# A mixture-of-experts layer whose expert rows are added in memory, the last block by a product

## The reference

```python
def moe_ffn(h, w_router, b_router, w_gate_up, b_gate_up, w_down, b_down):
    logits = (h @ w_router).astype(jnp.float32) + b_router
    topv, idx = lax.top_k(logits, TOP_K)            # 4 of 32 experts for each token
    gates = jax.nn.softmax(topv, axis=-1)
...
    def expert_block(args):
        xblk, e = args
        gu = xblk @ w_gate_up[e] + b_gate_up[e]
        gate = jnp.minimum(gu[:, :D_FF], SWIGLU_LIMIT)
        up = jnp.clip(gu[:, D_FF:], -SWIGLU_LIMIT, SWIGLU_LIMIT)
        act = (up + 1.0) * (gate * jax.nn.sigmoid(SWIGLU_ALPHA * gate))
        return act @ w_down[e] + b_down[e]
...
    out = jnp.zeros((t, d), jnp.float32).at[tbuf].add(ybuf.astype(jnp.float32) * wbuf[:, None])
    return out
...
        h2 = rmsnorm(x, norm_ffn_g).reshape(b * s, d)
        ff = moe_ffn(h2, w_router, b_router, w_gate_up, b_gate_up, w_down, b_down)
        x = x + ff.reshape(b, s, d).astype(x.dtype)
```

## Time and profile before

| | |
|---|---|
| three executions | 3075.31, 3075.50, 3072.84 us |
| median | 3075.31 us |
| profiled execution | 3074.51 us, its span 3072.7 us |
| TensorE busy | 2839.8 us (92% of the span) |
| VectorE busy | 1196.2 us (39%) |
| ScalarE busy | 802.5 us (26%) |
| GpSimd busy | 116.7 us (4%) |
| moved by DMA | 578.08 MB |
| granted TensorE clock, mean | 0.979 of full speed |

### The profile page before, as it was taken

The page is one execution under the profiler, slowest core; times in us unless marked ns, Lnnn a source line. Parts: engine busy times, 40 slices in busy tenths (PEclk is TensorE's granted clock), DMA queues, the critical chain, the costliest instruction groups (busy, mean ns, idle before and its releaser), DMA issues.

```text
span 3072.7 us, 42784 instructions
## 1 busy us (share of the span) xinstructions
PE 2839.8 (92%) x15464; PEld 1695.2 (55%) x15465; DVE 1196.2 (39%) x2551; ACT 802.5 (26%) x1607; POOL 116.7 (4%) x132
## 2 busy tenths in 40 slices
PE   8989889998999989899889779999999999999999
PEld 7874567753333333233333368575676596676774
DVE  6770674323212222122221166435333355444432
ACT  3221661111322222222222223423111224323111
POOL 0000100000000000000000000011000000110000
PEclk9999999997999999999999989999999999999999
DMA  4222002237999999999999552021321331122221
GB/s 175 83 69 69 15 1 96 83 138 298 395 419 401 425 426 403 418 395 411 423 406 397 205 200 97 28 93 36 102 83 55 99 101 55 54 74 76 82 69 69
DMA packets 119627, 578.08 MB, mean 188 GB/s; under 512 B 13933, under 2 KB 19437, under 8 KB 85712
## 3 DMA queue, kind: packets, MB, share of 16 engines
q1 hardware_dynamic: 110000, 559.37, 46.9%
q0 software_dynamic: 9504, 17.07, 1.5%
HBM read 572.97 MB, written 20.97 MB: 193 GB/s over the span
## 4 chain that ended last, share of the span: by engine, by line
PE 79%; DMA 11%; DVE 5%; ACT 2%; issue 2%; DVEq 1%; POOLq 0%; ACTq 0%; SPq 0%
PE banks L399 28%; PE banks L1547 11%; DMA arena<-in_w_up 10%; PE banks L336 8%; PE banks L1088 7%; PE banks L1588 5%; PE banks L841 4%; PE banks L1555 3%; PE banks L819 3%; PE banks L854 2%; PE banks L830 2%; PE banks L1594 2%; PE banks L275 1%; DVE arena L907 1%; PE banks L1527 1%
## 5 line engine op out<-in xcount | busy, mean ns | idle before, releaser
L399 PE MATMUL banks<-arena 128*128 128x256 f32 (+2 forms) x4256 | 916.3, 376 | 18.4 <-ACT arena L436 7.9
L399 PEld LDWEIGHTS banks<-arena 128*128 128x128 f32 x4256 | 795.7, 191 | 128.6 <-issue 21.9
L1547 PE MATMUL banks<-arena 128*64 128x512 f32 x2048 | 476.3, 610 | 67.8 <-DMA arena<-in_w_up 49.8
L1547 PEld LDWEIGHTS banks<-arena 128*64 128x64 f32 x2048 | 154.3, 139 | 343.8 <-issue 341.7
L436 ACT ACTIVATE arena<-banks 128x512 f32<-128x512 f32 (+2 forms) x152 | 89.1, 587 | 622.2 <-PE banks L399 622.2
L336 PE MATMUL banks<-arena 128*128 128x512 f32 x576 | 250.0, 592 | 0.0
L1588 PE MATMUL banks<-arena 128*64 128x512 f32 x1024 | 236.1, 599 | 0.0
L1689 DVE TENSOR_TENSOR arena<-banks,arena 128x512 f32<-128x512 f32 x64 | 44.3, 692 | 486.6 <-PE banks L1573 261.3
L452 DVE TENSOR_TENSOR arena<-banks,arena 128x512 f32<-128x512 f32 (+2 forms) x114 | 77.3, 678 | 383.2 <-PE banks L399 381.7
L1088 PE MATMUL banks<-arena 128*128 128x512 f32 x512 | 222.9, 592 | 3.7 <-DVEq L205 3.7
L384 DVE TENSOR_TENSOR arena<-arena 128x1024 f32<-128x1024 f32 (+2 forms) x152 | 182.4, 1200 | 21.8 <-issue 19.4
(11 more groups left out here) (218 smaller groups left out, 2389.1 us busy)
## 6 DMA issues: line engine op xcount, KB each, us to landing
arena<-in_w_up SPq DMA_DIRECT2D x128, 2048.0 KB, 23.4
arena<-in_w_down SPq DMA_DIRECT2D x128, 1024.0 KB, 21.5
arena<-in_w_in SPq DMA_DIRECT2D x76, 1024.0 KB, 5.0
arena<-in_w_out SPq DMA_DIRECT2D x12, 1024.0 KB, 5.0
arena<-in_w_branch SPq DMA_DIRECT2D x24, 512.0 KB, 4.7
arena<-expert_rows SPq DMA_DIRECT2D x4, 2048.0 KB, 14.5
arena<-in_w_in SPq DMA_DIRECT2D x2, 2048.0 KB, 10.0
arena<-in_w_in SPq DMA_DIRECT2D x4, 832.0 KB, 4.4
```

Source lines behind the costliest of these rows:

```text
L399: last = PE.matmul(PS[:, bank, t * width:(t + 1) * width], one[:, t * P:(t + 1) * P], other, start=(first and t == 0 and kk == 0), stop=(t ...
L1547: last = PE.matmul(PS[HB * s:HB * (s + 1), 4 + h], xT[:, k, 0:HB], gate_up(2 * h + s, k), start=(k == 0), stop=(k == 7))
```

## The change

The table of expert rows in memory is gone. In its place stands `x_sums`, 512 rows. The router stage writes x there. In the loop VectorE multiplies the rows of a block by their gates, and GpSimd adds them to `x_sums` with an indirect DMA whose operation is an addition, indexed by token. The last block isn't written: its rows lie in partitions 0 to 95 of `Y_`, the biases of the second matmul in partitions 96 to 127, and a matrix `SEL` holds in the same partitions the gate of each row at its token and the gates of all 32 experts for each token. One product with 128 steps for each half tile gives the contribution of the last block and of all biases. SyncE loads the sums back into `x3` once the write of the last block but one has landed, and VectorE adds the product. The gates of the list rows (`GLIST`) come from a second product of 16 steps in the router stage. The combine stage has no fence. Gathers and writes name 96 rows in place of 128.

```diff
-        YD = nc.dram_tensor("expert_rows", [S * TOPK, D], F32, kind="Internal").ap()
+        XD = nc.dram_tensor("x_sums", [S, D], F32, kind="Internal").ap()
...
+                sp.dma_start(v(Y_, D, NE, BS), A["b_down"]).then_inc(SEM["bdown_in"], 16)
...
-            G.indirect_dma_start(out=v(XG, D), out_offset=None, in_=H2D,
-                                 in_offset=bass.IndirectOffsetOnAxis(ap=v(TOK, 1).bitcast(U32), axis=0),
+            G.indirect_dma_start(out=v(XG, D, BS), out_offset=None, in_=H2D,
+                                 in_offset=bass.IndirectOffsetOnAxis(ap=v(TOK, 1, BS).bitcast(U32), axis=0),
...
             def pe_(pe, c):                                   # router stage
-                    last = PE.transpose(PS[0:NE, 3, tt * P:(tt + 1) * P], Gm[:, tt], ident)
+                    last = PE.matmul(PS[BS:P, 3, tt * P:(tt + 1) * P], Gm[:, tt], ident, start=True, stop=True, tile_position=(0, BS))
                 last.then_inc(SEM["gt_mm"], 1)
-                pe.wait_ge(SEM["gt_rdy"], up(1))
-                pe.wait_ge(SEM["bdown_in"], 16)
-                down_biases(0, 4)
-                down_biases(1, 6)
...
-                down_biases(2, 2)
-                pe.wait_ge(SEM["table_rdy"], up(1))
-                down_biases(3, 0)
+                for a_ in range(16):
+                    if a_ % 4 == 0:
+                        pe.wait_ge(SEM["gate_rows"], up(a_ // 4 + 1))
+                    last = PE.matmul(PS[0:BS, 2, 0:LISTS], gate_rows[:, a_], slots[:, a_].rearrange("p b e -> p (b e)"),
+                                     start=(a_ == 0), stop=(a_ == 15))
+                last.then_inc(SEM["gates_listed"], 1)
...
             def act_(act, c):                                 # router stage
+                for tt in range(TT):
+                    act.wait_ge(SEM["addr_rdy"], up(tt + 1))
+                    for a_ in range(4 * tt, 4 * tt + 4):
+                        last = AC.activation(gate_rows[:, a_], rows_at[:, a_, 0:BS], ACT.Copy, scale=per_slot[:, a_:a_ + 1])
+                    last.then_inc(SEM["gate_rows"], 1)
...
+                sp.dma_start(XD.rearrange("(t p) d -> p t d", p=P), x3).then_inc(SEM["sums_in"], 16)
...
             def sp_(sp, c):                                   # expert stage, behind its loop
                 sp.wait_ge(SEM["all_out"], up(1))
+                for tt in range(TT):
+                    sp.dma_start(x3[:, tt], XD[tt * P:(tt + 1) * P, :]).then_inc(SEM[f"comb{tt}"], 16)
+                sp.wait_ge(SEM["act_rdy"], up(2 * final + 2))
+                sp.wait_ge(SEM["gathered"], 16 * final + 32)
...
             def pe_(pe, c):                                   # expert stage
-                pe.wait_ge(SEM["bias_added"], up(2))
                 gather_T(1)
-                pe.wait_ge(SEM["bias_added"], up(4))
-                with pe.Fori(0, nb) as j:
+                pe.wait_ge(SEM["gt_rdy"], up(1))
+                pe.wait_ge(SEM["gates_out"], up(1))
+                with pe.Fori(0, final + 1) as j:
+                    few = entry(pe, FEW, j, 1)
                     pe.wait_ge(SEM["xt_free"], up(j + 1))
-                    few = entry(pe, FEW, j, 1)
...
+                pe.wait_ge(SEM["y_rdy"], up(final + 1))
+                for tt in range(TT):
+                    for n in range(2):
+                        last = PE.matmul(PS[:, SUMS[tt] + n], v(SEL + P * tt, P), v(Y_ + 512 * n, 512), start=True, stop=True)
+                    last.then_inc(SEM["comb_mm"], 1)
...
             def dve_(dve, c):                                 # expert stage, end of a block
-                    dve.wait_ge(SEM["rows_out"], up(j))
-                    V.tensor_copy(rsc, column(ALLR, here)).then_inc(SEM["rsc_rdy"], 1)
+                    if not ends:
+                        dve.wait_ge(SEM["rows_out"], up(j))
+                        V.tensor_copy(rsc, column(ALLT, here))
+                        dve.wait_ge(SEM["y_rdy"], up(j + 1))
+                        V.tensor_scalar(v(Y_, D, BS), v(Y_, D, BS), AR[0:BS, bass.ds(here + GLIST, 1)], None, ALU.mult)
+                        V.drain().then_inc(SEM["rsc_rdy"], 1)
+                with dve.Fori(0, final) as j:
+                    block(j, False)
+                block(final, True)
...
                 def scatter(n):
-                    pool.wait_ge(SEM["y_rdy"], up(n))
                     pool.wait_ge(SEM["rsc_rdy"], up(n))
-                    G.indirect_dma_start(out=YD, out_offset=bass.IndirectOffsetOnAxis(ap=rsc.bitcast(U32), axis=0),
-                                         in_=y, in_offset=None,
-                                         bounds_check=S * TOPK - 1, oob_is_err=False).then_inc(SEM["scattered"], 16)
+                    G.indirect_dma_start(out=XD, out_offset=bass.IndirectOffsetOnAxis(ap=rsc.bitcast(U32), axis=0),
+                                         in_=y, in_offset=None, bounds_check=S - 1, oob_is_err=False,
+                                         compute_op=ALU.add).then_inc(SEM["scattered"], 16)
...
             def dve_(dve, c):                                 # combine stage
                 for tt in range(TT):
                     dve.wait_ge(SEM[f"comb{tt}"], 16)
-                    for k in range(4):
-                        last = V.scalar_tensor_tensor(x3[:, tt], v(BIG + 4096 * tt + D * k, D), v(GATES + 4 * tt + k, 1),
-                                                      x3[:, tt], ALU.mult, ALU.add)
+                    dve.wait_ge(SEM["comb_mm"], up(tt + 1))
+                    last = V.tensor_tensor(x3[:, tt], x3[:, tt], PS[:, SUMS[tt]:SUMS[tt] + 2].rearrange("p a b -> p (a b)"), ALU.add)
                     last.then_inc(SEM["x_done"], 1)
...
-            return Stage(NORM, sp=sp_, dve=dve_, act=act_)
+            return Stage(NORM, dve=dve_, act=act_, fenced=False)
...
-            sp_after(sp, c)
```

More of the change, by code:

```diff
@@ L1261, in build @@
         R = SC
[L1262 removed]
+        GATES, BT = R + 2560, R + 3200
         WR = R + 3712
@@ L1275, in weights_in @@
             sp.dma_start(to, src).then_inc(SEM[f"ch{u}"], 16)
-        def down_biases(tt, bank):
-            for n in range(2):
-                last = PE.matmul(PS[:, bank + n], v(GT + tt * P, P, NE), v(BD + n * 512, 512, NE), start=True, stop=True)
-            last.then_inc(SEM["fin_mm"], 1)
         def gather(pool, n):
@@ L1456, in dve_ @@
                 V.tensor_copy(v(BE, 192, 1).bitcast(I32), PS[0:1, 1, 0:192])
-                V.tensor_copy(v(NBLK, 1, 1).bitcast(I32), cum[0:1, NE - 1:NE])
+                V.tensor_scalar(v(LAST, 1, 1).bitcast(I32), cum[0:1, NE - 1:NE], -1.0, None, ALU.add)
                 V.drain().then_inc(SEM["table_rdy"], 1)
+                dve.wait_ge(SEM["gates_listed"], up(1))
+                V.tensor_copy(v(GLIST, LISTS, BS), PS[0:BS, 2, 0:LISTS])
+                V.drain().then_inc(SEM["gates_out"], 1)
             def sp_(sp, c):
@@ L1506, in sp_ @@
                 norm_pre.lead(sp, c)
-                nb = nblocks(sp)
-                with sp.Fori(1, nb) as j:
+                final = last_block(sp)
+                with sp.Fori(1, final + 1) as j:
                     e = entry(sp, BE, j, NE - 1)
@@ L1626, in copy_T @@
                     AC.activation(v(XT, D), PS[:, 4:6].rearrange("p a b -> p (a b)"), ACT.Copy).then_inc(SEM["xt_free"], 1)
+                act.wait_ge(SEM["gates_listed"], up(1))
                 copy_T(1)
-                with act.Fori(0, nb) as j:
+                with act.Fori(0, final + 1) as j:
                     few = entry(act, FEW, j, 1)
@@ L1663, in act_ @@
                         rows_of_block(True)
+                AC.activation(v(SM + 320, 1), ident[:, 0:1], ACT.Sqrt)
             def dve_(dve, c):
-                nb = nblocks(dve)
-                for tt in range(TT):
-                    dve.wait_ge(SEM["fin_mm"], up(tt + 1))
-                    V.tensor_tensor(x3[:, tt], x3[:, tt], PS[:, (4, 6, 2, 0)[tt]:(4, 6, 2, 0)[tt] + 2].rearrange("p a b -> p (a b)"),
-                                    ALU.add).then_inc(SEM["bias_added"], 1)
+                final = last_block(dve)
@@ L1671, in dve_ @@
                 dve.wait_ge(SEM["gathered"], 16)
                 V.tensor_copy(tok, column(ALLT, entry(dve, BCOL, 1, LISTS - 1))).then_inc(SEM["tok_rdy"], 1)
-                with dve.Fori(0, nb) as j:
+                here_last = entry(dve, BCOL, final, LISTS - 1)
+                V.tensor_copy(v(TOKF, 1, BS), column(ALLT, here_last)[0:BS])
+                V.tensor_copy(v(TOKF + 5, 1, BS), AR[0:BS, bass.ds(here_last + GLIST, 1)])
+                V.drain()
+                for tt in range(TT):
+                    V.tensor_scalar(v(TOKF + 1 + tt, 1, BS), v(TOKF, 1, BS), float(PART), float(-P * PART * tt), ALU.mult, ALU.add)
@@ L1674, in dve_, with block @@
+                V.drain()
+                for tt in range(TT):
```

(22 more changed lines are left out.)

60 lines of the change are left out of this document (31 added, 29 removed).

## The result

The median is 3093.61 us (five executions, 3087.61 to 3097.72) against 3075.31 for the kernel before beside it: ratio 1.0058, 95% interval 1.0044 to 1.0073. The forecast was 3060, in a range to 3085. The change costs 18.3 us where it was to give 15. The profiled execution took 3095.15 us, its span 3093.3, 20.6 more than before.

What follows compares the result with a forecast made beforehand. The expert loop was held bound by TensorE in full blocks and DMA engines in runs of short ones, with an unshared chain behind it. 3075.3 - 26 (end) - 0.5 (start) + 11 (adding) = 3059.8 us; range 3046 to 3085.

Steps and rivals of the forecast that it cites:

- The end: From y's last copy to the last scaling: 41.6 us becomes 15.9; 26 us gained, bounds 24 to 28.
- the product: After the last block: tile 0 takes four instructions at 0.43 us each plus 0.35 for handing over, 2.1 us.
- late instruction fetch: After the last block: fetching the new code is hidden while ScalarE copies y for 3 us; uncovered, 2 us.
- The start: Before the loop: the gate product replaces four bias additions about one for one; -0.5 us, bounds -1.5 and +3.
- this mishap: At the start: the first gather, beside the new 2 MB write of x, could land 2 us later, partly covered.
- VectorE's gating in the loop: In each block: multiplying y by the gates takes 0.9 us before the write; hidden, otherwise some 2 us a block.
- the rival of the late landing: In the loop: adding writes land after 20 us, ScalarE's copy waits; about 3085. Shares 0.22 with the other slower rival.
- The rival that each row holds its engine for a trip to memory: In the loop: beyond 1.7 us a block, at most 12.6; kernel slower. Shares 0.22 with the late landing.
- the 19 that were counted: In the loop: saturated runs leading up to waits for weights take in about 19 of 31 blocks, 12 to 24.
- 64 x 0.158 / 16 = 0.63 us a block: In the loop: engines do each added row twice; 0.6 us over 19 blocks, 11 us. Forecast case's chance 0.42.
- my "middle" rival: In the loop: adding costs 1.1 to 1.7 us a block, 21 to 32 in all; 3070 to 3081, chance 0.15.
- 64 x 0.01 / 16 = 0.04 us: In each block: 64 rows no longer named, 32 each in gather and write, are packets of nothing; 0.04 us saved.

## Why the prediction was wrong

Three of the runs stand between the two kernels, so that from the second row on each step is one edit:

| from | to | us |
|---|---|---|
| kernel before, 3075.3 | changed kernel with plain writes, all of 128 names, 3050.9 | -24.4 |
| | writes of 96 names, 3043.0 | -7.9 |
| | writes that add, 3069.4 | +26.4 |
| | gathers of 96 names, 3093.6 | +24.2 |

The forecast of 3059.8 had -26.5 for the first row, next to nothing for the second and the fourth, and 11 for the third. So the miss of 33.8 us is 2.1 at the start and the end, 15.4 in the price of adding, and 24.2 in the names of the gathers, with 7.9 given back by the names of the writes.

**The end: right.** 24.3 us of the predicted 26. The loads of the sums left SyncE at 1775.17 and landed after 6.9 us at most, long before they were needed; the product took their place as what is late, and since it began 0.3 us behind the last copy, no late instruction fetch showed. The term that was off is the product: I took 0.43 us an instruction from a busy stretch, and after 3.3 us without a matmul its first five ran at a granted clock of 0.55.

**The start: right in its bounds.** Predicted -0.5, measured +1.0. The gate product took 5.44 of the 5.4 to 8.3 us allowed for it. The first gather stood beside the 2 MB write of x, and the first transposes waited 5.16 us for it. In the two versions that write into `expert_rows` and so don't write x, they waited 1.7 and 1.9 us and began 4.8 and 5.0 us behind the gather's issue; here it is 8.3, and 8.4 and 8.6 in two runs that write x and gather with 128 names. So this mishap, priced at up to 2, cost some 3.5. Without it the first product of the loop came at 720.1 and 720.9, about 3 us ahead of the kernel before: the small net figure was in part luck, the two misses having opposite signs.

**VectorE's gating in the loop: right.** Blocks with their weights in time keep their 23.7 and 37.5 us. So does the landing of the write: the rival of the late landing is out, by 12.9 us at most against 20. The rival that each row holds its engine for a trip to memory began beyond 1.7 us a block, with 6 rows one after another at 2.1 us each as its bound. An adding row took 0.33 us of its engine (worked out below), and the whole price of adding in this kernel is 26.4 us, or 1.4 a block over the 19 that were counted: it is out too.

**The addition: the row sized right, the price too small.** The step that failed is "64 x 0.158 / 16 = 0.63 us a block", with its 11 us, where 26.4 were measured. What an engine does for an adding row was sized well. Between 1260 and 1560 us the software queue takes, with 128 names, 4.4% with plain and 6.5% with adding writes, as these pairs of lines show, first plain, then adding:

```profile
q1 hardware_dynamic: 10906, 118.90, 95.5%
q0 software_dynamic: 2743, 5.01, 4.4%
```

```profile
q1 hardware_dynamic: 10375, 113.55, 92.7%
q0 software_dynamic: 2700, 4.89, 6.5%
```

2.1% of 4,800 us are 101 over some nine blocks, 11.2 us of engine time each, 0.70 when divided by 16. For each of 64 rows that is 0.175 us on top of 0.158: a row costs about twice. The Trainium skill, "Collectives: The Full Stack", section on the bandwidth ceiling, has a factor of 1.93 for the reduction of a collective, and the measured 2.1 comes near it.

What the division by 16 leaves out may be that the row work isn't even: if a chunk of weights lands only when the slowest of its engines is done, that engine sets the price. Adding costs, with everything else alike:

| names in the write | plain | adding | cost, us |
|---|---|---|---|
| 128 | 3050.9 | 3091.4 | 40.5 |
| 96 | 3043.0 | 3069.4 | 26.4 |
| 64 | 3037.0 | 3050.4 | 13.5 |

The runs with 128 and 96 names add exactly the same rows; the names left out are those of empty places. If only the time of the rows themselves counted, evenly spread, the first two costs would be equal, and they differ by 14 us. Short blocks fill places 0 to 63 and full ones at most 0 to 95. If 128 names go to the engines eight by eight, as whole partitions do, half of the engines get all the rows of a short block, eight each; with 96 names it can be six, with 64 four. The costs go as 8 to 5.2 to 2.7, in that order but steeper than 8 to 6 to 4 (the last leaves rows out besides). The landings of the writes go the same way: at the median 12.4, 10.7 and 9.1 us adding, and 10.5, 9.5 and 8.1 plain, for 128, 96 and 64 names. The Trainium skill, "DMA: Bandwidth & Descriptors", section "The descriptor swizzle", has partitions 0 to 63 of a transfer to 128 partitions on engines 0 to 7. That fits, though it isn't said of indirect writes.

The queues allow a second reading. From the third write of rows to that of block 30 all these runs move the same 355 MB of weights. What adding puts to the length of this stretch can be split by the shares of the two queues (the share of each queue times the length, so within 1 to 2 us; two shares can sum to a little over 100%, which makes the last column negative):

| names in the write | longer by, us | packets of the software queue | packets of the weights | engines without a packet, or the excess over 100% |
|---|---|---|---|---|
| 128 | 39.2 | 19.5 | 12.1 | 7.6 |
| 96 | 24.3 | 19.4 | 10.4 | -5.5 |
| 64 | 13.9 | 17.7 | -1.0 | -2.7 |

The rows' own time is nearly the same each time, 0.6 to 0.7 us a block over 28 blocks, as forecast; with 64 names the whole cost is no more than that. What grows with the names are the weights' packets, from 38.2 to 38.8 and 39.2 us of an engine per MB with adding writes (plain 38.3, 38.4 and 38.7), and at 128 names time in which engines have nothing to do. Engines without work fit an uneven deal; longer packets of weights fit it only if they are longer for having to wait on the loaded engines, and would fit as well if adding rows slowed the memory for all. The profile doesn't show single engines. So that the cost depends on the names is shown, and the reason is argued. By the prediction's own count of 19 saturated blocks, 26.4 us are 1.4 us a block, which would have been my "middle" rival; 40.5 are 2.1.

**The names: the failed step is "64 x 0.01 / 16 = 0.04 us".** I priced the 64 names as packets of nothing and gave them no other effect. They have two, of opposite sign. Left out of the write they give 7.9 to 12.2 us (four pairs: 3050.9 to 3043.0, 3075.6 to 3067.4, 3104.5 to 3093.7, and 3056.3 to 3044.1). With adding writes it is 22.0, since there the names also make the addition cheaper. Left out of the gather they cost 24.2 and 26.7 in the changed kernel (adding and plain) and 29 in the one before, and not by their number: gathers of 112, 96 and 64 names take 3104.5, 3104.5 and 3094.4 us there against 3074.3 to 3075.6 for 128 (with 64, a few per cent of the rows aren't read either). The queue lines place the cost in the weights' own transfers, 39.4 to 39.9 us of an engine per MB between 1260 and 1560 us in every run with gathers of fewer than 128 names, adding or plain, and 38.1 to 38.6 in every plain run with 128. With adding writes and 128-name gathers it is 38.1 to 39.2.

Why, I can only argue. The weights go to all 128 partitions. A gather of 128 names could deal its rows over the engines in the way the weights are dealt, so that each engine keeps to its own partitions; with any other number it deals them otherwise, and two engines write to the same part of on-chip memory at once. The section "The descriptor swizzle" of the same page of the Trainium skill has each engine write one port in a 128-partition transfer, and says so of that shape only; no run here shows a port. Such a collision would not touch the writes, which read on-chip memory. That the names of the gathers cost 24 to 29 us, and in the weights' transfers, is shown; why stays open.

Put together, without either naming the prediction's own kernel would have been 3050.9 + 40.5 = 3091.4. So the addition is enough for the sign; with the names of the write it becomes cheap enough for a gain of 6 us, and the names of the gather take it back with 18 more. Undoing the addition alone, or the gathers' names alone, brings the change to 3069.7 or 3069.4. Both undone, and the sums made by VectorE under the last block, it is 3044.1.

## What to carry to other kernels

Where a loop waits for transfers that are spread over all DMA engines, the price of small transfers beside them can be more than their total divided by 16: here adding rows cost 13.5 to 40.5 us for nearly the same work. Test it by changing which rows are named, at the same number of rows moved. An edit that names fewer rows is an edit of its own: it has to be priced and run apart from what it comes with, in each direction, since here its two halves had effects of -8 and +29 on the kernel before. And a fixed cost at the end of a loop can often be put under the last iteration with the data path left alone: plain writes with the loads behind each freed chunk gave 31 us, the addition in memory with the same names 6, although the end of the adding version was 6 us shorter still.

## What the runs showed of the hardware

- An indirect gather of 112, 96 or 64 names beside streaming loads of 128 partitions made these take 39.8 to 39.9 us of an engine per MB for 38.5, with the gather's own landing little changed at the median (11.3, 10.9 and 9.5 us for 10.7 at 128). A 96-name indirect write did not (38.4).
- An adding indirect DMA costs about twice the engine time of a plain one for each 4 KB row, and its landing is 1.0 to 1.9 us longer at the median with the same names. With nearly all rows out of bounds the kernel took 3048.4 us, 21 under plain writes that move theirs, and the software queue 2.7% for 4.7%.
- The name of an empty place has a price in an indirect write: at 128, 96 and 64 names the changed kernel with plain writes took 3050.9, 3043.0 and 3037.0 us (the last writes fewer rows as well).
